# Second feed-forward layer of a transformer block in two column passes, with 14 of 64 pairs of weight row blocks multiplied by seven block products in place of eight

## The reference

```python
def sq_relu_mlp(h, w1, w2):
    return jnp.square(jax.nn.relu(h @ w1)) @ w2
...
        x = x + g1 * y
        h2 = modulate(rmsnorm(x, norm2_g[l]), sh2, sc2)
        x = x + g2 * sq_relu_mlp(h2, w1[l], w2[l])
    return rmsnorm(x, final_norm_g)
```

## Time and profile before

| | |
|---|---|
| median of 3 runs | 1499.62 us (1499.24 to 1499.99) |
| profiled execution, device time | 1499.28 us |
| its span, first to last instruction | 1497.5 us |
| TensorE busy, mean granted clock | 98% of the span, 0.998 |
| DVE busy | 66% |
| ACT busy | 44% |
| POOL busy | 3% |
| mean DMA share of 16 engines | about 70% |

### The profile page before, as it was taken

One profiled execution on the slowest core, in us unless ns is written; L12 is line 12 of the kernel. 1 busy time (PEld: TensorE's weight loads), 2 busy tenths in 40 slices (PEclk: granted clock), 3 DMA queues, 4 the chain that ended last, 5 costly groups with the idle time before them and its releaser, 6 DMA issues.

```text
span 1497.5 us, 19363 instructions
## 1 busy us (share of the span) xinstructions
PE 1467.6 (98%) x7297; PEld 1209.8 (81%) x7297; DVE 992.1 (66%) x1166; ACT 665.5 (44%) x900; POOL 49.9 (3%) x32
## 2 busy tenths in 40 slices
...
GB/s 368 382 362 250 267 260 207 227 185 165 233 205 241 205 235 366 327 290 362 234 199 168 173 237 308 267 269 306 186 168 211 195 193 192 191 195 196 188 192 98
DMA packets 123037, 355.73 MB, mean 238 GB/s; under 512 B 10962, under 2 KB 11986, under 8 KB 122322
## 3 DMA queue, kind: packets, MB, share of 16 engines
...
## 4 chain that ended last, share of the span: by engine, by line
PE 88%; DVE 5%; issue 2%; ACT 2%; DMA 2%; ACTq 0%; POOL 0%; POOLq 0%; DVEq 0%
PE bank L1553 21%; PE bank L1555 20%; PE bank L1554 20%; PE bank L1839 14%; PE bank L1842 7%; PE bank L1709 2%; PE bank L1682 1%; DVE wl L1120 1%; DMA raw<-in_w_ada 1%; ACT wh L692 1%; PE bank L1584 1%; PE bank L1672 1%; DVE acc L1151 1%; DMA ident<-in_identity 1%; PE bank L1635 0%
## 5 line engine op out<-in xcount | busy, mean ns | idle before, releaser
L1120 DVE TENSOR_TENSOR wl<-raw,wh 128x1024 fp32r<-128x1024 f32 x451 | 555.5, 1243 | 365.4 <-ACT wh L692 364.2
L692 ACT ACTIVATE wh<-raw 128x1024 fp32r<-128x1024 f32 x452 | 472.8, 1059 | 476.5 <-PE bank L1555 288.1
L1839 PE MATMUL bank<-h2S,wh 128*128 128x512 f32 x896 | 245.0, 395 | 0.8 <-DVE wl L1120 0.7
L1553 PE MATMUL bank<-wh,hT 128*128 128x512 f32 x512 | 207.0, 404 | 0.5 <-DVE wl L1120 0.5
L1555 PE MATMUL bank<-wh,hT 128*128 128x512 f32 x512 | 200.3, 391 | 0.0
L1554 PE MATMUL bank<-wl,hT 128*128 128x512 f32 x512 | 199.9, 390 | 0.0
L1553 PE MATMUL bank<-wh,hidS 128*128 128x512 f32 x496 | 193.1, 389 | 0.0
L1555 PE MATMUL bank<-wh,hidS 128*128 128x512 f32 x496 | 193.1, 389 | 0.0
L1554 PE MATMUL bank<-wl,hidS 128*128 128x512 f32 x496 | 193.1, 389 | 0.0
L1839 PEld LDWEIGHTS bank<-h2S,wh 128*128 128x128 f32 x896 | 153.3, 189 | 21.5 <-DVE wl L1120 0.9
L1151 DVE SCALAR_TENSOR_TENSOR acc<-raw,cc,acc 128x1024 f32<-128x1024 f32 x120 | 153.5, 1279 | 0.0
...
## 6 DMA issues: line engine op xcount, KB each, us to landing
raw<-in_w SPq DMA_DIRECT2D x256, 512.0 KB, 4.4
raw<-in_w_ada SPq DMA_DIRECT2D x192, 512.0 KB, 5.7
raw<-in_w_in SPq DMA_DIRECT2D x128, 512.0 KB, 4.6
raw<-in_w_attn_o SPq DMA_DIRECT2D x32, 512.0 KB, 6.2
raw<-in_w_out SPq DMA_DIRECT2D x32, 512.0 KB, 6.1
raw<-in_w_fourier SPq DMA_DIRECT2D x16, 512.0 KB, 6.2
xt<-in_x SPq DMA_DIRECT2D x2, 1024.0 KB, 6.2
ct<-in_ctx SPq DMA_DIRECT2D x2, 1024.0 KB, 10.6
```

The lines of the kernel that those rows point to most:

```text
L692: nc.scalar.activation(slot, raw[:, s % RAW, :], ACT.Copy).then_inc(wh_done, 1)
L1120: nc.vector.tensor_tensor(lo, raw[:, s % RAW, :], hi.bitcast(F32), ALU.subtract)\
L1553: nc.tensor.matmul(bank[b][:], a_hi, w_hi, start=first, stop=False)
L1839: nc.tensor.matmul(out[:], wh[:, slot, cols_f[f]], h2S[:, block, :, :].rearrange("p v t -> p (v t)"), start=(block == 0), stop=False)
```

## The change

The layer runs in two passes, one for each 1024 columns, over 32 pairs of row blocks: 64 pairs, each of two tiles (2i and 2i + 1), the first pass in banks 0 to 3. Tile n is now row block n % 64 of column half n // 64.

A plain pair is done as before: eight block products. As each pass needs the split hidden values, they are split once for every plain pair, 50 times in all. In 14 pairs, seven in each pass (`SEVEN_AT`), the 2 x 2 block product (two token blocks x two row blocks, times two row blocks x two halves of 512 columns) is made of seven block products. It needs seven left operands: three blocks of `hid` itself and four sums of them, which POOL makes (`aF`), and seven right operands: three half tiles and four sums of half tiles, which DVE makes (`tF`). All are split by ACT (`aH`, `tH`) and DVE (`aL`, `tL`); `aF`, `tF` and their parts have one buffer each. Three of the seven products add to banks 0, 2 and 1; four have their own sums in banks 4 to 7 over the seven pairs of the pass, and are then added to the result (`combine`, in the plain pairs behind the last such pair).

At the start of the second pass DVE empties banks 0 to 3 (`taken`, with the gate) and adds them to x1 (`added`). ACT squares those parts during the second pass, DVE multiplies them with `fgrow` (`prescaled`). The fetch of `fgrow` moves ahead of the tiles of w2. The loops are written out. The tail deals with four parts in place of eight; the last four tiles are done with the banks of the first token block first. `lastH` and `lastL` are not used by this layer any more.

The diff, cut to its core:

```diff
+PARTS = [(0, 0, 0), (0, 0, 1), (0, 1, 0), (0, 1, 1), (1, 0, 0), (1, 1, 0), (1, 0, 1), (1, 1, 1)]
...
+SEVEN_AT = ((2, 5, 9, 12, 16, 19, 23), (0, 3, 7, 10, 14, 17, 21))
+NP = DFF // P // 2
+PAIRS, PLAIN = [], []
+for _c in range(2):
+    for _p in range(NP):
+        _seven = SEVEN_AT[_c].index(_p) + len(SEVEN_AT[0]) * _c if _p in SEVEN_AT[_c] else None
+        PAIRS.append((_c, _p, _seven, len(PLAIN)))
+        if _seven is None:
+            PLAIN.append(len(PAIRS) - 1)
+SEVENS = [i for i, pair in enumerate(PAIRS) if pair[2] is not None]
+COMBINE_AT = {2: "first", 3: "second", 4: 0, 5: 1, 6: 2, 7: 3}
+TAIL = 2 * NP - 2
...
-            with nc.sync.Fori(0, N2 // 8) as g:
+            for n in range(N2):
+                col, k = divmod(n, DFF // P)
+                sp.wait_ge(wl_done, W2 + n - RAW + 1)
+                sp.dma_start(raw[:, (S2 + n) % RAW, :], w2[k * P:(k + 1) * P, col * NC:(col + 1) * NC]).then_inc(raw_full[(S2 + n) % RAW], 16)
...
+            pool.wait_ge(hid_ready, 4 + 2 * (N1 - 1))
+            for i in SEVENS:
+                _, p, s, _ = PAIRS[i]
+                k1, k2 = 2 * p, 2 * p + 1
+                if s:
+                    pool.wait_ge(a_lo, 3 * s)
+                then(nc.gpsimd.tensor_tensor(aF[:, 0, :], hid[:, k2, P:T], hid[:, k1, P:T], ALU.subtract))
+                nc.gpsimd.tensor_tensor(aF[:, 2, :], hid[:, k1, 0:P], hid[:, k1, P:T], ALU.subtract)
+                then(nc.gpsimd.tensor_tensor(aF[:, 1, :], aF[:, 0, :], hid[:, k1, 0:P], ALU.add))
+                nc.gpsimd.tensor_tensor(aF[:, 3, :], hid[:, k2, 0:P], aF[:, 1, :], ALU.subtract).then_inc(a_sum, 1)
...
+            def tile_hi(n, width=NC):
+                s = S2 + n
+                act.wait_ge(raw_full[s % RAW], 16 * (s // RAW + 1))
+                act.wait_ge(gemm_done, M2 + n - SPL + 1)
+                nc.scalar.activation(wh[:, n % SPL, 0:width], raw[:, s % RAW, 0:width], ACT.Copy).then_inc(wh_done, 1)
+            def plain_hi(i, p, x):
+                if x >= 2:
+                    act.wait_ge(gemm_done, M2 + 2 * PLAIN[x - 2] + 2)
+                nc.scalar.activation(hidS[0][:, x % 2, :, :], hid[:, 2 * p:2 * p + 2, :], ACT.Copy).then_inc(hs_hi, 1)
+                tile_hi(2 * i)
+                tile_hi(2 * i + 1)
+            def seven_hi(i, p, s):
+                if s == 0:
+                    act.wait_ge(row_done, 4)
+                else:
+                    act.wait_ge(gemm_done, M2 + 2 * SEVENS[s - 1] + 2)
+                nc.scalar.activation(aH[:, 4:6, :], hid[:, 2 * p:2 * p + 2, 0:P], ACT.Copy).then_inc(a_hi, 1)
+                nc.scalar.activation(aH[:, 6, :], hid[:, 2 * p + 1, P:T], ACT.Copy).then_inc(a_hi, 1)
+                act.wait_ge(a_sum, s + 1)
+                nc.scalar.activation(aH[:, 0:4, :], aF[:], ACT.Copy).then_inc(a_hi, 1)
+                tile_hi(2 * i, HC)
+                tile_hi(2 * i + 1)
+                for j in range(2):
+                    act.wait_ge(wl_done, W2 + 2 * i + j + 1)
+                    nc.scalar.activation(tH[:, 2 * j:2 * j + 2, :], tF[:, 2 * j:2 * j + 2, :], ACT.Copy).then_inc(t_hi, 1)
...
+            for i, (ps, p, s, x) in enumerate(PAIRS):
+                if s is None:
+                    plain_hi(i, p, x)
+                else:
+                    seven_hi(i, p, s)
+                if i == 1:
+                    square_sum(N1 - 1, 1)
+                if p == SEVEN_AT[ps][-1] + 2:
+                    copy_p1(ps)
+                if ps == 1 and 3 <= p < 7:
+                    last_square(p - 3)
...
+            last_square(4)
+            last_square(5)
+            act.wait_ge(rs2_ready, 1)
+            last_scaled(0, 4)
+            last_scaled(2, 4)
+            last_square(6)
+            last_square(7)
             act.wait_ge(rs2_ready, 2)
...
+            def plain_lo(i, p, x):
+                dve.wait_ge(hs_hi, x + 1)
+                nc.vector.tensor_tensor(hidS[1][:, x % 2, :, :], hid[:, 2 * p:2 * p + 2, :],
+                                        hidS[0][:, x % 2, :, :].bitcast(F32), ALU.subtract).then_inc(hs_lo, 1)
+                for n in (2 * i, 2 * i + 1):
+                    split_lo(W2 + n + 1, S2 + n, wh[:, n % SPL, :], wl[:, n % SPL, :])
+            def seven_lo(i, p, s):
+                n1, n2 = 2 * i, 2 * i + 1
+                r1, r2 = raw[:, (S2 + n1) % RAW, :], raw[:, (S2 + n2) % RAW, :]
+                dve.wait_ge(a_hi, 3 * s + 2)
+                for part, src in ((slice(4, 6), hid[:, 2 * p:2 * p + 2, 0:P]), (slice(6, 7), hid[:, 2 * p + 1:2 * p + 2, P:T])):
+                    nc.vector.tensor_tensor(aL[:, part, :], src, aH[:, part, :].bitcast(F32), ALU.subtract).then_inc(a_lo, 1)
+                dve.wait_ge(a_hi, 3 * s + 3)
+                nc.vector.tensor_tensor(aL[:, 0:4, :], aF[:], aH[:, 0:4, :].bitcast(F32), ALU.subtract).then_inc(a_lo, 1)
+                dve.wait_ge(wh_done, W2 + n1 + 1)
+                nc.vector.tensor_tensor(wl[:, n1 % SPL, 0:HC], r1[:, 0:HC], wh[:, n1 % SPL, 0:HC].bitcast(F32), ALU.subtract)
+                if s:
+                    dve.wait_ge(t_hi, 2 * s)
+                nc.vector.tensor_tensor(tF[:, 0, :], r1[:, 0:HC], r1[:, HC:NC], ALU.add)
+                dve.wait_ge(raw_full[(S2 + n2) % RAW], 16 * ((S2 + n2) // RAW + 1))
+                nc.vector.tensor_tensor(tF[:, 1, :], r1[:, HC:NC], r2[:, HC:NC], ALU.add).then_inc(wl_done, 1)
+                dve.wait_ge(wh_done, W2 + n2 + 1)
+                nc.vector.tensor_tensor(wl[:, n2 % SPL, :], r2, wh[:, n2 % SPL, :].bitcast(F32), ALU.subtract)
+                dve.wait_ge(wl_done, W2 + n1 + 1)
+                then(nc.vector.tensor_tensor(tF[:, 2, :], tF[:, 0, :], r2[:, HC:NC], ALU.add))
+                nc.vector.tensor_tensor(tF[:, 3, :], tF[:, 2, :], r2[:, 0:HC], ALU.add).then_inc(wl_done, 1)
+                dve.wait_ge(wl_done, W2 + n2 + 1)
+                for j in range(2):
+                    dve.wait_ge(t_hi, 2 * s + j + 1)
+                    part = slice(2 * j, 2 * j + 2)
+                    nc.vector.tensor_tensor(tL[:, part, :], tF[:, part, :], tH[:, part, :].bitcast(F32), ALU.subtract).then_inc(t_lo, 1)
+            def combine(c, step):
+                if step == "first":
+                    dve.wait_ge(p1_copied, c + 1)
+                    then(nc.vector.tensor_tensor(tF[:, 1, :], tF[:, 0, :], bank[5][:], ALU.subtract))
+                    then(nc.vector.tensor_tensor(tF[:, 2, :], tF[:, 1, :], bank[6][:], ALU.add))
+                elif step == "second":
+                    then(nc.vector.tensor_tensor(tF[:, 1, :], tF[:, 1, :], bank[7][:], ALU.add))
+                    nc.vector.tensor_tensor(tF[:, 3, :], tF[:, 2, :], bank[7][:], ALU.add).then_inc(combined, 1)
+                else:
+                    if c == 0 and step == 0:
+                        dve.wait_ge(row_done, 4)
+                    dve.wait_ge(combined, c + 1)
+                    i = PARTS.index((c, step // 2, step % 2))
+                    then(nc.vector.tensor_tensor(scr2[:, step, :], tF[:, step, :], gate_cols(i), ALU.mult))
+                    part = last_part(x1, i)
+                    then(nc.vector.tensor_tensor(part, part, scr2[:, step, :], ALU.add if step < 2 else ALU.subtract))
+            def taken(i):
+                nc.vector.tensor_tensor(scr2[:, i, :], bank[i][:], gate_cols(i), ALU.mult).then_inc(z_free, 1)
+            def added(i):
+                part = last_part(x1, i)
+                dve.wait_ge(z_free, i + 1)
+                nc.vector.tensor_tensor(part, part, scr2[:, i, :], ALU.add).then_inc(x2_ready, 1)
+            def gated(i):
+                dve.wait_ge(z_full, i - 3)
+                then(nc.vector.tensor_tensor(scr2[:, i - 4, :], last_bank(i)[:], gate_cols(i), ALU.mult))
+                part = last_part(x1, i)
+                nc.vector.tensor_tensor(part, part, scr2[:, i - 4, :], ALU.add).then_inc(x2_ready, 1)
...
+            for i, (ps, p, s, x) in enumerate(PAIRS):
+                if s is None:
+                    plain_lo(i, p, x)
+                else:
+                    seven_lo(i, p, s)
+                if i == 0:
                     add_halves(N1 - 1, 1)
+                if p - SEVEN_AT[ps][-1] in COMBINE_AT:
+                    combine(ps, COMBINE_AT[p - SEVEN_AT[ps][-1]])
+                if ps == 1 and p == 0:
+                    dve.wait_ge(gemm_done, M2 + 2 * NP)
+                    for n in range(4):
+                        taken(n)
+                if ps == 1 and p == 1:
+                    for n in range(4):
+                        added(n)
+                if ps == 1 and p == 9:
+                    dve.wait_ge(fg_in, 16)
+                    dve.wait_ge(x2_ready, 4)
+                if ps == 1 and 9 <= p < 13:
+                    prescaled(p - 9)
+            gated(4)
+            gated(5)
+            gated(6)
             last_mean(0)
+            dve.wait_ge(x2_ready, 7)
+            prescaled(6)
+            gated(7)
             dve.wait_ge(rs2_ready, 1)
```

(124 more changed lines are left out.)

129 lines of the change are left out of this document (47 added, 82 removed).

## The result

The changed kernel takes 1503.15 us (median of 10 runs, 1501.68 to 1504.87) against 1499.7 (1499.24 to 1500.05) before: ratio 1.0023, 95% interval 1.0013 to 1.0033. It is 3.45 us slower; forecast were 2.3 us faster, and a range up to 1502.5.

The account below looks back on a forecast made before the run. TensorE's matmul columns were taken to bound the kernel (busy 98%). Saving, first seven pair, gap-four pairs, second pass, tail: -9.5 + 3.0 + 0.6 + 3.0 + 0.6 = -2.3, so 1497.3 us; range 1493.5 to 1502.5.

Parts of the forecast that it names:

- What it saves: In the layer's 14 seven pairs, 42 matmuls fewer at 0.2267 us each: 9.52 us saved, 1494 matmuls left.
- First seven pair: At pair 2, TensorE waits for POOL's first sums and then DVE's chain: stall 3.0 us, bounds 1.5 and 4.5.
- POOL's hold on DVE: POOL's four sums beside a seven pair's chain take 0.2 us each from DVE, 0.8 in all; bounds 0 and 1.4.
- The slack of 0.87: At gap-four pairs, DVE's first tL was to end 0.87 us before TensorE needs it.
- the gap-four pairs: Seven pairs behind three plain ones, six in all: 0.1 us stall each, 0.6 together, bounds 0 and 4.4.
- rival (b): POOL holds DVE 0.4 us per operation, gap-four pairs stall 0.73 each: 1504.6 us, deciding from 0.22 each; chance 0.12.
- Start of the second pass: At pairs 32 to 35, DVE falls behind emptying and adding four banks: 3.0 us of waits, bounds 1.9 and 4.8.
- Handoffs: Between engines throughout the layer, each handoff was taken to cost 0.03 to 0.04 us.
- T: The time at which TensorE gets to a pair; a plain pair takes 5.44 us, a seven pair 4.76.
- the last pairs: At the layer's end, the last hidS waits for pair 61, its two tiles ready 0.2 us late.
- rival (c): Handoffs of 0.12 us in the dense chain, so gap-four pairs stall 0.8 each: 1500 to 1501.5 us; chance 0.16.
- Tail: After TensorE's end, ACT gets to the last square 0.4 us later; with the last pairs 0.6, bounds 0.4 and 0.8.

Follow-up runs that it names:

- e8: The changed kernel with seven pairs at 3, 6, ... and 0, 4, 7, ..., POOL's sums later, and in the tail the mean ahead of part 6: 1491.93 us.
- e6: The changed kernel, its seven pairs where they are, but POOL only writes a constant and reads nothing, the left sums left out: 1495.13 us.
- e2: e1, but POOL's four operations only write a constant and read nothing from SBUF, so the left sums are left out: 1494.02 us.
- the second profile: The changed kernel, unchanged, executed and profiled once more: 1503.29 us.
- e3: e1 with the second pass's seven pairs at 0, 4, 7, ... in place of 0, 3, 7, ...: 1494.37 us.
- e4: The changed kernel with no seven pair at all, two passes with eight block products everywhere: 1502.73 us.
- e1: The changed kernel with the first pass's seven pairs at 3, 6, 9, ... in place of 2, 5, 9, ...: 1496.25 us.

## Why the prediction was wrong, point by point

**What it saves** was right: 1494 matmuls, at 0.2267; e8's layer is 338.5 + 1.2.

**First seven pair: the step that failed.** Stall 3.0, bounds 1.5 and 4.5; measured 5.8. The gaps are 4.15: POOL's four sums (0.87, 1.32, 0.63 and 0.46, where I had 0.35, by the price of a memset's columns, and a wait for each) ended 3.5 after ACT's square in place of 3.0, DVE's chain from there on took 7.3 in place of 6.8, and 0.3 had been rounded off. The rest, 1.7, is the clock, for which the sum had no term at all. The text called it open; it should have been in the high end. DVE's own share, 1.5 in the low end, is 1.2 in e6.

**POOL's hold on DVE.** 0.2 for each operation, 0.8 a pair; it is 0.25 to 0.26, 1.0 a pair. The rows I had showed no hold, but they could not: the DVE instruction that followed the POOL one undelayed, `qT<-bank,qT`, takes one input from PSUM. The slack of 0.87 was also too large. Where nothing holds DVE (pair 53, the gap-four pairs of e2), its first tL ends 0.71 before the matmul that needs it, and where TensorE waits 0.05 before, so the slack is 0.66. A hold of 1.05 exceeds it by 0.4, and with 0.11 for the matmul behind the wait that is the 0.52. It came only where POOL's first sum took 0.85: twice at gap-four pairs, in the second profile four times, where I had 0.1 on average: 1.05 and 2.1 against 0.6. The average was near for the first profile by luck, since I had neither the size nor the two ways. The rival (b) had the mechanism and the point from which it decides (0.22), but put the high price of 0.4 on it.

**Start of the second pass.** 3.0 forecast, 3.4 measured; near in its sum, less so in its parts: 0.4 forecast at pair 33 and 0.95 measured, and 0.5 at pair 32, for which the sum had no term (it is a pair of the kind just told). Without POOL's reads e2 has 2.2, where the low end had 1.9. e3 showed its larger part, pair 3, to be a question of place.

**Handoffs.** I took T from the distances of starts. But a product is done only 0.39 after its last start by the record, not 0.23 (in the earlier trace rows ACT's copy that waits for one begins 0.43 after it), and a matmul that ends a wait and the one behind it cost 0.08 to 0.11 more. That would fit the last pairs, which stall 0.55 where I had 0.2 (the second to last hidS starts only then), and e4's bank, which costs 1.1 for 0.9. It is rival (c) in small: no longer handoffs, but two ends of each that were left out. The experiments do not part it from the sum of small errors in DVE's chain.

**Tail.** 0.4 forecast, 0.7 measured, 0.5 of it by the cause named (e8); the other 0.2 stays open.

**The sum.** Stalls of 6.8 us with the last pairs against 10.8, tail 0.4 against 0.7, and 0.1 to 0.9 ahead of the layer (by the pairs of profiles). The kernel was lost at one pair: without its 6 us the rest would have come to 1497, as e1 shows with 1496.25. The sum's own high end, 1504.6, held the measured time; the stated range left it out, since it cut rival (b). That end would have been right only by luck: it had 4.5 for the first seven pair, which took 5.8, and 4.4 for the gap-four ones, which took 1.05 to 2.1.
